# Loading the norm weights as one row and spreading them with GpSimd, and packing the gate columns, in the setup of a hybrid encoder block

## The reference

```python
h = rmsnorm(x, norm_w)                      # x * rsqrt(mean(x*x) + eps) * norm_w
p = h @ w_in                                # all projections at once
# columns of w_in: qkv (1536), z (512), b (8), a (8), fox q, k, v, z (4 * 512), f (8), gates (2048)
y_a = gated_deltanet(...)                   # 8 heads, chunks of 64; b, a are its gate logits
y_b = forgetting_attention(...)             # 8 heads; f is its forget-gate logit
m = sigmoid(g_a) * (y_a @ w_up_gdn) + sigmoid(g_b) * (y_b @ w_up_fox)
out = rmsnorm(x + m @ w_out, final_norm_w)
```

## Time and profile before

| | before |
|---|---|
| device time, median of 3 | 949.03 us |
| lowest and highest of 3 | 947.95, 949.48 us |
| profiled execution: span | 945.6 us |
| profiled execution: its own device time | not given apart from the three above |
| TensorE busy | 925.3 us (98%) |
| VectorE, ScalarE busy | 610.6 us (65%), 471.8 us (50%) |
| GpSimd busy | 19.7 us (2%) |
| granted TensorE clock | 1.0 of full in nearly all of the span |

### The profile page before, as it was taken

One profiled execution on the slowest core, in us unless ns is written; L12 is line 12 of the kernel. 1 busy time (PEld: TensorE's weight loads), 2 busy tenths in 40 slices (PEclk: granted clock), 3 DMA queues, 4 the chain that ended last, 5 costly groups with the idle time before them and its releaser, 6 DMA issues.

```text
span 945.6 us, 15912 instructions
## 1 busy us (share of the span) xinstructions
PE 925.3 (98%) x6380; PEld 700.9 (74%) x6380; DVE 610.6 (65%) x982; ACT 471.8 (50%) x842; POOL 19.7 (2%) x28
## 2 busy tenths in 40 slices
PE   5999999999999999999999999999999999999997
PEld 4778787888888876676766666666667888888885
DVE  7487568799999934454496786767862433246252
ACT  7555654532866625532756547556554442334131
POOL 1000002020000000000000000000000000000000
PEclk9999999999999999999999999999999999999999
DMA  8111351249323393322553325234125323123162
GB/s 251 45 49 45 96 178 48 68 143 228 100 90 104 107 271 89 102 74 91 139 181 94 109 101 168 102 102 123 35 68 178 108 71 94 51 112 112 45 192 75
DMA packets 115744, 104.87 MB, mean 111 GB/s; under 512 B 34192, under 2 KB 95760, under 8 KB 115288
## 3 DMA queue, kind: packets, MB, share of 16 engines
q1 hardware_dynamic: 104008, 80.27, 30.6%
q10 hardware_dynamic: 10512, 19.40, 5.6%
q0 software_dynamic: 1152, 4.19, 1.3%
HBM read 76.84 MB, written 27.00 MB: 110 GB/s over the span
## 4 chain that ended last, share of the span: by engine, by line
PE 45%; DVE 3%; ACT 1%; DMA 1%; issue 1%; SPq 0%; DVEq 0%; ACTq 0%
PE pj L2182 6%; PE pj L2184 5%; PE pj L2183 5%; PE pc L2315 4%; PE pa L2281 3%; PE pa L2250 1%; PE pj L2193 1%; PE pj L2195 1%; PE pj L2194 1%; PE pb L2341 1%; PE pb L2330 1%; PE pc L2450 1%; PE pc L2449 1%; PE pb L2450 1%; PE pb L2449 1%; PE pa L2450 1%
## 5 line engine op out<-in xcount | busy, mean ns | idle before, releaser
L144 PE MATMUL pj<-h_hi,w_hi 128*128 128x512 f32 x504 | 203.6, 404 | 0.5 <-DVE w_lo L132 0.5
L145 PE MATMUL pj<-h_lo,w_hi 128*128 128x512 f32 x504 | 196.9, 391 | 0.0
L146 PE MATMUL pj<-h_hi,w_lo 128*128 128x512 f32 x504 | 196.5, 390 | 0.0
L144 PEld LDWEIGHTS pj<-h_hi,w_hi 128*128 128x128 f32 x504 | 94.5, 187 | 23.9 <-issue 1.1
L146 PEld LDWEIGHTS pj<-h_hi,w_lo 128*128 128x128 f32 x504 | 94.6, 188 | 20.4
L145 PEld LDWEIGHTS pj<-h_lo,w_hi 128*128 128x128 f32 x504 | 94.7, 188 | 18.0 <-issue 0.2
L2182 PE MATMUL pj<-h_hi,w_hi 128*128 128x512 f32 x248 | 101.2, 408 | 0.3 <-PEq L315 0.3
L2184 PE MATMUL pj<-h_hi,w_lo 128*128 128x512 f32 x248 | 96.8, 390 | 0.0
L2183 PE MATMUL pj<-h_lo,w_hi 128*128 128x512 f32 x248 | 96.7, 390 | 0.0
L2182 PEld LDWEIGHTS pj<-h_hi,w_hi 128*128 128x128 f32 x248 | 46.5, 188 | 19.6 <-issue 10.1
L572 ACT ACTIVATE xc<-pj 128x512 f32<-128x512 f32 x39 | 23.3, 597 | 72.4 <-PE pj L146 71.8
(11 more groups left out here) (366 smaller groups left out, 1858.2 us busy)
## 6 DMA issues: line engine op xcount, KB each, us to landing
w_raw<-in_w_in SPq DMA_DIRECT2D x48, 512.0 KB, 4.4
fox_scratch<-xc ACTq DMA_DIRECT2D x39, 256.0 KB, 2.7
qkv<-in_x SPq DMA_DIRECT2D x8, 512.0 KB, 6.8
fa<-rows_scratch POOLq DMA_DIRECT2D x8, 512.0 KB, 4.8
rv<-fr_scratch SPq DMA_DIRECT2D x16, 256.0 KB, 4.0
ma<-m_scratch SPq DMA_DIRECT2D x8, 512.0 KB, 4.4
rv<-in_w_out SPq DMA_DIRECT2D x8, 512.0 KB, 3.7
w_raw<-in_x SPq DMA_DIRECT2D x8, 512.0 KB, 4.5
```

Source lines behind the costliest of these rows:

```text
L144: nc.tensor.matmul(o, w_hi[:, slot, k], h_hi[:, k, cols], start=(k == 0), stop=False)
L145: nc.tensor.matmul(o, w_hi[:, slot, k], h_lo[:, k, cols], start=False, stop=False)
L146: last = nc.tensor.matmul(o, w_lo[:, slot, k], h_hi[:, k, cols], start=False, stop=(k == KT - 1))
```

## The change

The norm weights are loaded as one row of 4 KB into partition 0 of `att` (which is free in the setup), and GpSimd copies that row to all 128 partitions of `nw_bc` once it is there; VectorE waits for the copy. The gate columns b and a, which lie side by side in w_in, are loaded together, f alone, both packed into columns 0 to 23 of `w_raw` slot 0. `w_hi` and `w_lo` are computed from those 24 columns a k-slice and written straight to the places 0, 32 and 64. The zeros between are now set in `w_hi` and `w_lo` themselves, by GpSimd, after the spread. What GpSimd zeroed in `w_raw` falls away, and with it SyncE's wait ahead of the gate loads.

```diff
-        SMALL_DMAS = 3
+        SMALL_DMAS = 2
...
+        nw_row = att[0:1, 0:S]
...
+        packed_rows = w_raw[:, 0, :, 0:3 * H].rearrange("p k (g c) -> p k g c", c=H)
+
+        def spread_rows(w):
+            return w[:, 0, :, 0:96].rearrange("p k (g c) -> p k g c", c=32)[:, :, :, 0:H]
...
@@ SyncE
-                sp.wait_ge(zeroed, 1)
-                sp.dma_start(w_raw[:, 0, :, 0:H], w_view[:, :, COL_B:COL_B + H]).then_inc(w_loaded[0], 16)
-                sp.dma_start(w_raw[:, 0, :, 32:32 + H], w_view[:, :, COL_A:COL_A + H]).then_inc(w_loaded[0], 16)
-                sp.dma_start(w_raw[:, 0, :, 64:64 + H], w_view[:, :, COL_F:COL_F + H]).then_inc(w_loaded[0], 16)
+                sp.dma_start(w_raw[:, 0, :, 0:2 * H], w_view[:, :, COL_B:COL_B + 2 * H]).then_inc(w_loaded[0], 16)
+                sp.dma_start(w_raw[:, 0, :, 2 * H:3 * H], w_view[:, :, COL_F:COL_F + H]).then_inc(w_loaded[0], 16)
...
-                sp.wait_ge(zeroed, 2)
+                sp.wait_ge(zeroed, 1)
@@ GpSimd
-                nc.gpsimd.memset(w_raw[:, 0], 0.0).then_inc(zeroed, 1)
                 nc.gpsimd.memset(rows_in[:, :], 0.0).then_inc(zeroed, 1)
                 link(nc.gpsimd.memset(ident[:, :], 0.0))
                 link(nc.gpsimd.affine_select(ident[:, :], ident[:, :], pattern=[[-1, P]], base=0,
                                              channel_multiplier=1, compare_op=ALU.not_equal, fill=1.0))
+                pool.wait_ge(nw_loaded, 16)
+                nc.gpsimd.partition_broadcast(nw_bc, nw_row).then_inc(nw_spread, 1)
+                nc.gpsimd.memset(w_hi[:, 0, :, 0:ROWS].bitcast(F32), 0.0).then_inc(zeroed, 1)
+                nc.gpsimd.memset(w_lo[:, 0, :, 0:ROWS].bitcast(F32), 0.0).then_inc(zeroed, 1)
@@ ScalarE
-                act.dma_start(nw_bc, norm_w[0, :].partition_broadcast(P)).then_inc(nw_loaded, 16)
+                act.dma_start(nw_row, norm_w[0:1, :]).then_inc(nw_loaded, 16)
...
                 act.wait_ge(w_loaded[0], loads_of(0, 0))
-                nc.scalar.activation(w_hi[:, 0, :, 0:ROWS], w_raw[:, 0, :, 0:ROWS], ACT.Copy).then_inc(w_hi_done, 1)
+                act.wait_ge(zeroed, 2)
+                nc.scalar.activation(spread_rows(w_hi), packed_rows, ACT.Copy).then_inc(w_hi_done, 1)
@@ VectorE
-                dve.wait_ge(nw_loaded, 16)
+                dve.wait_ge(nw_spread, 1)
...
                 dve.wait_ge(w_hi_done, 1)
-                nc.vector.tensor_tensor(w_lo[:, 0, :, 0:ROWS], w_raw[:, 0, :, 0:ROWS], w_hi[:, 0, :, 0:ROWS].bitcast(F32),
+                dve.wait_ge(zeroed, 3)
+                nc.vector.tensor_tensor(spread_rows(w_lo), packed_rows, spread_rows(w_hi).bitcast(F32),
                                         ALU.subtract).then_inc(w_ready, 1)
@@ TensorE
-                pe.wait_ge(zeroed, 2)
+                pe.wait_ge(zeroed, 1)
```

More of the change, by code:

```diff
@@ L55, in program @@
     N_FOX = 4 * PAIRS
+    assert COL_A == COL_B + H and H == 8
     assert S == 2 * HALF and NT == 8 and KT == 8 and PAIRS == 4 and QKV_T == 12
@@ L189, in program @@
         nw_loaded = sem("nw_loaded")
+        nw_spread = sem("nw_spread")
         rstd_step = sem("rstd_step")
```

## The result

| | before | after |
|---|---|---|
| device time, median of 4 | 948.49 us | 963.44 us |
| lowest and highest | 947.77, 949.48 us | 962.68, 965.88 us |
| ratio to before, 95% interval | 1 | 1.0159 [1.0145, 1.0174] |
| span of the profiled execution | 945.6 us | 960.9 us (its device time 962.68) |
| first scaled tile on VectorE (S) | 7.81 | 21.12 |

What follows compares the result with a forecast made beforehand. The prediction took TensorE as the bound, busy 925.3 of 945.6 us, with the setup acting through the first projection matmul. One fetch moved that from 17.21 to 20.6: 949.03 + 3.4 = 952.4 us, range 947.5 to 959.

Steps and rivals of the forecast that it cites:

- The mechanism: In the setup, GpSimd fetches a routine ahead of the spread, delaying VectorE's first scaled tile; first projection matmul 3.4 us later.
- the chain from the first scaled tile to the first matmul: Setup path through scaled tile 3, h_lo and w_lo to the first projection matmul, put at S + 8.55 us.
- the count of fetches: On GpSimd in the setup, one fetch of 8.3 us, ahead of the spread; none ahead of the mask selection.
- The size of one fetch: Ahead of GpSimd's spread, between 0.24 and 8.3 us; 8.3 taken, the longest landing of transfers issued then.
- the forecast's own 950.5 to 954: Span of the single-fetch forecast: fetch from 1.6 taking 7.3 us, to fetch from 3.5 with w_lo at 0.75.
- Rival C: GpSimd's old state is restored behind the last barrier, adding at least 5.2 us: 957.6 us; chance 0.26.
- The 3.4 us around the span: Median 949.03 us over the span of 945.6, taken as room for an ending cost the trace does not show.
- x tile 0: First x tile's load in the setup lands at about 4.5, 1.4 us earlier, without the 0.5 MB of norm weights.
- w_lo: VectorE's last setup step before the first projection matmul: 0.35 instead of 0.75 us, so 0.4 us earlier.
- rival B: Nothing is fetched ahead of GpSimd's spread, so the setup gains 1.8 us in all: 947.2 us; chance 0.13.
- rival A: GpSimd's fetch ends sooner, 5.2 us; first matmul 0.65 us earlier to 1.35 later, 948.4 to 950.4 us; chance 0.16.
- One thing for one: Every microsecond's shift of the first projection matmul, 17.21 us into the span, counts one for one in the final time.

Runs made afterwards that it cites:

- e6: The changed kernel plus, as GpSimd's very last instruction, an unread elementwise add of one number that fetches the old set back; 953.27 us, ratio 1.0046.
- e3: The kernel before plus, as GpSimd's very last instruction, a spread of one number that nothing reads; 952.52 us, ratio 1.0044.
- e1: The changed kernel with GpSimd's spread of the norm weights moved ahead of the mask selection that makes the identity; 947.59 us, ratio 0.9991.
- e7: The kernel of e1 plus eight unread transposes of the identity in TensorE's gap between x tiles 2 and 3; 947.55 us, ratio 0.9995.
- e4: The changed kernel with the spread done by two TensorE matmuls into PSUM instead of by GpSimd; 946.68 us, ratio 0.9979.
- e2: The packed gate columns alone, with norm weights loaded to all partitions as in the kernel before; 948.25 us, ratio 0.9999.
- e8: The kernel of e2 plus eight unread transposes of the identity in the same TensorE gap as in e7; 948.35 us, ratio 0.9996.

## Why the prediction was wrong

**The mechanism was right as far as it went.** A long gap stands ahead of the spread, VectorE and then TensorE start late, and the delay goes through to the end. The reading that rested on it also held: the chain from the first scaled tile to the first matmul was put at 8.55 us and is 8.59 in the changed kernel (21.12 to 29.71) and in e6 (13.15 to 21.74), with the wait for statistics 3 where it was said to be.

**The step that failed is the count of fetches.** The prediction let the mask selection keep its gap: "The mask selection that began at 2.23 and took 0.28 then ends near 1.6". It charged one fetch, ahead of the spread, and put what a second would cost at nothing. The row of 0.24 us was a fact about an execution that followed another of the same kernel, not about the instruction. With the spread in the program, the selection still asks for its own set, finds the other one in place and costs a fetch of its own (8.57 and 9.93 us in two profiles; 11.45 in e3). A sign of it was in the trace of the kernel before: the MODIFY_POOL_CONFIG pair ahead of that selection. e6 separates the two: without the fetch ahead of the selection the time is 953.27 us, inside the forecast's own 950.5 to 954; with it, 963.

**The size of one fetch was low by 1.5 to 1.9 us, and its start too late.** 8.3 us were taken for it; the three ahead of the setup's spread took 9.84, 9.96 and 10.23. In e6 it begins at 1.86, right behind the selection and before the row is in, where the prediction took the middle of 1.6 and 3.5. The two errors pull against each other, so that S = 12.05 for a single fetch came as near to the 13.15 of e6 as it did is in part luck. The Trainium skill (GPSIMD Engine Reference, section 2.1, Instruction dispatch) gives about 6 us (5.95), without a visible instruction. The traces agree in so far as no row shows the load itself; on its size they don't: 8.07 is the shortest of all eight gaps quoted here.

**Rival C named the right thing at the wrong place.** It had something "put back", as a cost behind the last barrier that would show in the time and not in the span. Nothing is put back at the end: the span grew by 15.3 us in the profiled execution and the time with it. The price is paid at the start of the next execution. The 3.4 us around the span, which were its support, were a misreading: they set the span of one execution against the median of others, and in every recorded execution the two differ by 1.8 us.

**The smaller terms held.** x tile 0 came 1.5 us earlier (1.4 forecast), w_lo took 0.35, the spread 1.30 (1.2 forecast), the row was in by 2.3 in e1 and by 3.4 in e7 (3.5 forecast). w tile 1 went out at 4.57, not 6.5, and was hidden as said. That 1.8 us are to be had without fetches was the estimate for rival B; e4 measures 2.0 us by its ratio (0.21%; its median is 1.5 us lower), e1 0.9 us by its ratio, with an interval that includes no gain. One sum was slightly off: rival A's later end, S = 9.9, gives a first matmul 1.24 us later and not 1.35.

**One thing for one was almost right.** The first matmul was 12.5 and 14.25 us late in the two profiles of the changed kernel, the ends 15.3 and 15.6, with scatter between.

## What to carry to other kernels

Before an instruction is moved to GpSimd, ask whether the engine runs anything of its kind already: in these runs a routine that was not in place cost 8 to 11 us ahead of its first use, and the set that it left behind cost as much again ahead of the first routine of the next execution, if that one asked for another set. The view of a source line shows, by MODIFY_POOL_CONFIG, where the program asks. If such a routine is wanted, put it first in the program and use nothing outside its set, or fetch the old set back where the engine is idle; and look for an engine that needs no fetch, as TensorE did here with two matmuls. A gap of zero ahead of an instruction may say what ran before it, in this execution or the one before, and need not hold once the program is changed.

## What the runs showed of the hardware that was not expected

- GpSimd's state outlives the program: a spread at 641 us delays the first selection of the next execution by 11.2 us (11.45 against 0.24).
- The set that holds the spread also serves the mask selections: one starts at 3.45 us, directly behind the spread, in e1, and the later selections of the changed kernel have no gap. A selection that comes first in the program asks for another set all the same (8.57 us in the kernel after, 11.45 in e3).
- Asking for the set that is in place costs less than 0.1 us: the pair at 2.1 to 2.2 us in the kernel before, the selection at 2.23.
- Fetch gaps: 8.07 and 9.28 us at 641 and 648 us into the kernel, and 8.57 to 11.45 us in the setup, beside the loads of x and w. Neither place is quiet: the DMA engines are 91% and 87% busy in the first two gaps and 61% to 96% in the others, and the gap with 61% took 10.23 us. How much the traffic costs stays open; no run has a fetch beside idle DMA engines.
- TensorE's granted clock fell from 2.4 to 1.2 GHz for 3.4 us in e1 and e2, behind idle times of 0.5 to 0.9 and 1.4 us among fast transposes, and not in e7 and e8, where eight transposes stood in the longer one. In the kernel before it did not fall there; its third group of transposes still took 1.55 us (1.16 in e1 and e2), and its idle times were shorter (0.48 and 1.02 us). The granted clock does not show when TensorE had sped up at first: it reads 1.00 over the first transposes too, although eight of them take 1.94 us there, as they do at 0.50 in e2.
